# Attention of eight running samples: scores of samples 3 to 8 from rounded parts and rests

## What is computed

```python
def mla_sample(h, pos, c_ckv, c_kpe, ...):
    q_lat = jnp.einsum('bqhn,lhn->bqhl', q_nope, w_uk)
    s_past = (jnp.einsum('bqhl,bkl->bhqk', q_lat, c_ckv)
              + jnp.einsum('bqhr,bkr->bhqk', q_pe, c_kpe))
    s_new = (jnp.einsum('bqhl,bkl->bhqk', q_lat, ckv)
             + jnp.einsum('bqhr,bkr->bhqk', q_pe, kpe))
    sc = jnp.concatenate([s_past, s_new], axis=-1).astype(jnp.float32) * MLA_SCALE
    p = jax.nn.softmax(sc, axis=-1).astype(ckv.dtype)
    o_lat = (jnp.einsum('bhqk,bkl->bqhl', p[..., :past], c_ckv)
             + jnp.einsum('bhqk,bkl->bqhl', p[..., past:], ckv))
    o = jnp.einsum('bqhl,lhv->bqhv', o_lat, w_uv)...
```

## Time and profile before

| | us |
|---|---|
| median of 3 runs (1609.39 to 1609.46) | 1609.39 |
| span of the profiled execution | 1608.3 |
| PE busy in it | 1600.9 |
| DVE busy | 820.0 |
| ACT busy | 597.6 |
| POOL busy | 268.1 |

### The profile page before, as it was taken

How to read it: one execution, slowest core, us unless ns; L and a number is a source line. 1 busy time by engine, 2 the same in 40 slices (tenths; PEclk the granted TensorE clock), 3 DMA queues, 4 the chain that set the end, 5 groups by cost and what they waited for, 6 DMA issues and landing times.

```text
span 1608.3 us, 24111 instructions
## 1 busy us (share of the span) xinstructions
PE 1600.9 (100%) x9172; PEld 1532.5 (95%) x9172; DVE 820.0 (51%) x968; ACT 597.6 (37%) x770; POOL 268.1 (17%) x267
## 2 busy tenths in 40 slices
PE   9999999999999999999999999999999999999998
PEld 9999999988999999999999999898989899999987
DVE  6544344864454444445444344674747576444422
ACT  6333222574343333234333223424343354333322
POOL 0111122530121110221111032303030312111000
PEclk9999999999999999999999999999999999999999
DMA  7444344564244443454444345566575755444332
GB/s 218 121 121 130 105 126 135 173 206 148 58 126 130 130 127 94 126 150 131 130 123 120 104 125 186 204 219 228 198 245 172 254 179 147 130 130 130 113 125 103
DMA packets 322273, 238.03 MB, mean 148 GB/s; under 512 B 8560, under 2 KB 287280, under 8 KB 322096
## 3 DMA queue, kind: packets, MB, share of 16 engines
q1 hardware_dynamic: 321936, 236.86, 48.3%
q10 hardware_dynamic: 288, 0.50, 0.1%
HBM read 215.34 MB, written 20.94 MB: 147 GB/s over the span
## 4 chain that ended last, share of the span: by engine, by line
PE 98%; DVE 1%; ACT 1%; issue 0%; DMA 0%; ACTq 0%; DVEq 0%
PE bank L168 26%; PE bank L170 26%; PE bank L169 26%; PE bank L489 2%; PE bank L488 2%; PE bank L487 2%; PE bank L1666 1%; PE bank L1665 1%; PE bank L1664 1%; PE bank L1073 1%; PE bank L396 1%; PE bank L1702 1%; PE bank L1777 1%; PE bank L1733 1%; PE bank L1692 0%; PE bank L917 0%
## 5 line engine op out<-in xcount | busy, mean ns | idle before, releaser
L145 DVE TENSOR_TENSOR WL<-RAW,WH 128x2048 fp32r<-128x2048 f32 (+3 forms) x191 | 401.8, 2105 | 296.3 <-ACT WH L138 295.6
L138 ACT ACTIVATE WH<-RAW 128x2048 fp32r<-128x2048 f32 (+3 forms) x191 | 330.0, 1730 | 561.9 <-PE bank L170 479.5
L168 PE MATMUL bank<-XH,WH 128*128 128x384 f32 x1368 | 458.4, 335 | 0.0
L170 PE MATMUL bank<-XH,WL 128*128 128x384 f32 x1368 | 457.1, 334 | 0.0
L169 PE MATMUL bank<-XL,WH 128*128 128x384 f32 x1368 | 457.0, 334 | 0.0
L168 PEld LDWEIGHTS bank<-XH,WH 128*128 128x128 f32 x1368 | 256.8, 188 | 3.4 <-issue 3.1
L169 PEld LDWEIGHTS bank<-XL,WH 128*128 128x128 f32 x1368 | 256.8, 188 | 0.2
L170 PEld LDWEIGHTS bank<-XH,WL 128*128 128x128 f32 x1368 | 256.8, 188 | 0.0
L653 POOL TENSOR_TENSOR si<-si,rsb 128x384 f32<-128x384 f32 x88 | 94.3, 1072 | 626.4 <-ACT si L524 591.8
L168 PE MATMUL bank<-AH,WH 128*128 128x384 f32 x528 | 176.4, 334 | 0.0
L169 PE MATMUL bank<-AL,WH 128*128 128x384 f32 x528 | 176.4, 334 | 0.0
(11 more groups left out here) (307 smaller groups left out, 1960.3 us busy)
## 6 DMA issues: line engine op xcount, KB each, us to landing
RAW<-w_ffn_gate_dram SPq DMA_DIRECT2D x86, 512.0 KB, 4.0
RAW<-w_ffn_up_dram SPq DMA_DIRECT2D x86, 512.0 KB, 5.2
RAW<-w_ret_in_dram SPq DMA_DIRECT2D x48, 512.0 KB, 4.8
RAW<-w_ffn_down_dram SPq DMA_DIRECT2D x48, 384.0 KB, 4.0
st<-state_ret_dram SPq DMA_DIRECT2D x32, 512.0 KB, 6.9
new_state_sample_dram<-st SPq DMA_DIRECT2D x32, 512.0 KB, 6.6
RAW<-w_ffn_down_dram SPq DMA_DIRECT2D x48, 320.0 KB, 3.3
RAW<-w_ffn_down_dram SPq DMA_DIRECT2D x22, 512.0 KB, 4.3
```

Of the source, the lines that this page charges most:

```text
L138: ins = act.activation(dst(WH), src, ACT.Copy)
L145: ins = dve.tensor_tensor(dst(WL), src, dst(WH).bitcast(F32), ALU.subtract)
L168: pe.matmul(ps, wh, xh, start=first, stop=False)
L170: return pe.matmul(ps, wl, xh, start=False, stop=last)
```

## The change

- Keys of a sample now lie in one tile of three parts, two latent and one rotated (the 64 rotated rows twice, on both halves of the partitions), 128x3x528, and come in one transfer. There are four tiles in place of three.
- Both score banks now hold 272 keys. The banks are pairs that one instruction can read (`bank_pair`): samples take the up banks and the down banks in turn; the mixings use `norm_ps` and `misc_ps`.
- Samples 0 and 1 keep full-precision scores. For samples 2 to 7 (the third to the eighth) ACT rounds the keys (`keys_hi`) and the latent queries (`queries_hi`), DVE subtracts what was rounded off (`key_rest`, `query_rest`), in place, and PE makes 16 rounded matmuls of 272 columns for each sample. The rotated queries carry rounded part and rest on the two halves of the partitions.
- ACT rounds the keys of sample b+2 behind the exponentials of b. Behind them come the copies of the turned probabilities of b-2, and then the copy of the latents of b-3, which was DVE's.
- DVE takes one maximum over both banks; ahead of that of sample b stands the rest of the keys of b+1. ACT makes two exponentials in place of three.
- SP's queue issues all key loads first and then the latent rows of samples 4 to 7.
- Semaphores are merged (`consts_set`, `m_ps`, `m_negmax`).

The diff, cut to what is spoken of:

```diff
-                sp.dma_start(ktc[b % N_KT][:, :, 0:PAST_LEN], a["ckvT"][b]).then_inc(sem(f"kt_in{b % N_KT}"), 16)
-                sp.dma_start(ktp[b % N_KT][:, 0:HP], a["kpeT"][b]).then_inc(sem(f"kt_in{b % N_KT}"), 16)
+                sp.dma_start(keys_in[b % N_KT][:, :, 0:PAST_LEN], a["keysT"][b]).then_inc(sem(f"kt_in{b % N_KT}"), 16)
...
+                for b in range(N_KT, DEC_BATCH):
+                    sp.wait_ge(sem("m_sscores"), 2 * (b - N_KT + 1))
+                    self.load_keys(sp, b)
+                for b in range(NCB, DEC_BATCH):
+                    sp.wait_ge(sem("m_smixed"), b - NCB + 1)
+                    sp.dma_start(cc[:, b % NCB, :, :], a["ckv"][b]).then_inc(sem(f"cc_in{b % NCB}"), 16)
...
-            SA, SB, MIX = up_ps, (down_ps[0], norm_ps), (down_ps[1], misc_ps)
-            LAST_MIX = (misc_ps, norm_ps)
+            SCORES, MIX = bank_pair[1:3], (norm_ps, misc_ps)
+            LAST_MIX = (misc_ps, up_ps[0])
...
-                pe.matmul(sa, q0, latent[:, 0, HP:], start=True, stop=False)
-                pe.matmul(sa, q1, latent[:, 1, HP:], start=False, stop=False)
-                pe.matmul(sb_, q0, latent[:, 0, 0:HP], start=True, stop=False)
-                pe.matmul(sb_, q1, latent[:, 1, 0:HP], start=False, stop=False)
-                pe.matmul(sa, qr[0:ROPE, :], rotated[0:ROPE, :], start=False, stop=True).then_inc(sem("m_sscores"), 1)
-                pe.matmul(sb_, qr[ROPE:P, :], rotated[ROPE:P, 0:HP], start=False, stop=True).then_inc(sem("m_sscores"), 1)
+                if b >= SPLIT:
+                    n, hi, lo = b - SPLIT, key_hi[b % 2], key_lo[b % N_KT]
+                    for i, cols in enumerate(HALVES):
+                        for t in range(KV):
+                            pe.matmul(ps[i], lat_hi[:, t, n, :], hi[:, t, cols], start=(t == 0), stop=False)
+                            pe.matmul(ps[i], lat_hi[:, t, n, :], lo[:, t, cols], start=False, stop=False)
+                            pe.matmul(ps[i], lat_lo[:, t, b, :], hi[:, t, cols], start=False, stop=False)
+                        pe.matmul(ps[i], rot_q[:, n, :], hi[:, KV, cols], start=False, stop=False)
+                        pe.matmul(ps[i], rot_q[:, n, :], lo[:, KV, cols], start=False, stop=True).then_inc(sem("m_sscores"), 1)
+                    return
...
+                def keys_hi(b):
+                    act.wait_ge(sem(f"kt_in{b % N_KT}"), 16 * (b // N_KT + 1))
+                    act.wait_ge(sem("m_kt_new"), 2 * (b + 1))
...
+                    act.activation(key_hi[b % 2][:, :, :], keys_in[b % N_KT][:, :, :], ACT.Copy).then_inc(sem("m_split"), 1)
...
                 turned(MLA_HEADS - 1)
+                keys_hi(SPLIT)
+                act.wait_ge(sem("m_lat"), 4 * KV)
+                queries_hi(SPLIT, SPLIT + 3)
                 mixed(MLA_HEADS - 1)
...
                 for b in range(DEC_BATCH):
                     if b == 1:
                         new_rows()
+                    act.wait_ge(sem("m_snegmax"), 2 * (b + 1))
+                    act.wait_ge(sem("m_zero"), b + 1)
+                    scores = self.SCORES[b % 2]
+                    new = PAST_LEN + b * DEC_SEQ
+                    past = ps_[:, b % 2, PAST].rearrange("p (i n) -> p i n", i=2)
+                    for j, (dst, src) in enumerate(((past, scores[:, :, 0:HP]), (ps_[:, b % 2, new:new + DEC_SEQ], scores[:, 1, HP:KW]))):
+                        act.activation(dst, src, ACT.Exp, bias=stat[:, b % 2, 1:2], scale=MLA_SCALE,
+                                       accum_out=stat[:, b % 2, 2 + j:3 + j]).then_inc(sem("m_sexp"), 1)
+                    if b == 0:
+                        queries_hi(SPLIT + 3, DEC_BATCH)
+                    elif b + 2 < DEC_BATCH:
+                        keys_hi(b + 2)
                     if b >= 2:
                         turned_probs(b - 2)
-                    act.wait_ge(sem("m_snegmax"), b + 1)
-                    act.wait_ge(sem("m_zero"), b + 1)
-                    sa, sb_ = self.SA[b % 2], self.SB[b % 2]
-                    new = PAST_LEN + b * DEC_SEQ
-                    for j, (dst, src) in enumerate(((slice(0, HP), sa[:, 0:HP]), (slice(HP, PAST_LEN), sb_[:, 0:HP]),
-                                                    (slice(new, new + DEC_SEQ), sa[:, HP:KW]))):
-                        act.activation(ps_[:, b % 2, dst], src, ACT.Exp, bias=stat[:, b % 2, 2:3], scale=MLA_SCALE,
-                                       accum_out=stat[:, b % 2, 4 + j:5 + j]).then_inc(sem("m_sexp"), 1)
+                    if b >= 3:
+                        latents(b - 3)
...
+                def key_rest(b):
+                    dve.wait_ge(sem("m_split"), (1, 4, 5, 6, 7, 8)[b - SPLIT])
+                    dve.tensor_tensor(key_lo[b % N_KT][:, :, :], keys_in[b % N_KT][:, :, :], key_hi[b % 2][:, :, :].bitcast(F32),
+                                      ALU.subtract).then_inc(sem("m_rests"), 1)
...
                 for b in range(DEC_BATCH):
                     st = stat[:, b % 2, :]
-                    for j, (ps, n) in enumerate(((self.SA[b % 2], KW), (self.SB[b % 2], HP))):
-                        dve.wait_ge(sem("m_sscores"), 2 * b + 1 + j)
-                        dve.tensor_reduce(st[:, j:j + 1], ps[:, 0:n], AX.X, ALU.max).then_inc(sem("m_smax"), 1)
...
+                    if 2 <= b < DEC_BATCH - 1:
+                        key_rest(b + 1)
+                    dve.wait_ge(sem("m_sscores"), 2 * (b + 1))
+                    dve.tensor_reduce(st[:, 0:1], self.SCORES[b % 2][:, :, 0:KW], AX.XY, ALU.max).then_inc(sem("m_snegmax"), 1)
+                    dve.wait_ge(sem("m_snegmax"), 2 * b + 1)
+                    dve.tensor_scalar(st[:, 1:2], st[:, 0:1], -MLA_SCALE, None, ALU.mult).then_inc(sem("m_snegmax"), 1)
+                    if b == 0:
+                        key_rest(SPLIT)
+                        query_rest(SPLIT)
+                    elif 2 <= b < DEC_BATCH - 1:
+                        query_rest(b + 1)
+                    dve.wait_ge(sem("m_sexp"), 2 * (b + 1))
+                    dve.tensor_reduce(st[:, 4:5], st[:, 2:4], AX.X, ALU.add).then_inc(sem("m_ps"), 1)
...
-                    if b >= 3:
-                        mixed(b - 3)
-                for b in range(DEC_BATCH - 3, DEC_BATCH - 1):
-                    mixed(b)
...
+                for b in range(SPLIT, DEC_BATCH):
+                    if b + 1 < DEC_BATCH:
+                        new_keys(b + 1)
+                    zeros(b)
```

More of the change, by code:

```diff
@@ L83, in stream_kernel @@
         var = sb("var", [P, T])
+        with ExitStack() as r:
+            sq_split = sb("sq_split", [P, 2 * T], F32R, r)
         sq = sb("sq", [P, 2, T])
@@ L89, in stream_kernel @@
         accl = sb("accl", [P, T], F32R)
+        with ExitStack() as r:
+            bank_pair = [r.enter_context(nc.psum_tensor(f"bank_pair{i}", [P, 2, 512], F32)) for i in range(4)]
         bank = [ctx.enter_context(nc.psum_tensor(f"bank{i}", [P, 512], F32)) for i in range(8)]
@@ L711, in stream_kernel @@
             mcos, msin = mtab[:, 0:T], mtab[:, T:2 * T]
-            shared = sb("shared", [P, MLA_HEADS * T + KV * D_MODEL], F32, r)
+            widths = (MLA_HEADS * T + KV * D_MODEL, MLA_HEADS * T + MLA_HEADS * KV_LORA, 2 * KT, KV * DEC_BATCH * MLA_HEADS * DEC_SEQ)
+            with ExitStack() as r0:
+                whole = sb("whole", [P, sum(widths)], F32, r0)
+            with ExitStack() as r0:
+                split = sb("split", [P, sum(widths)], F32R, r0)
+            (shared, late, kt, lat), (shared_r, late_r, kt_r, lat_r) = (
+                [x[:, sum(widths[:i]):sum(widths[:i + 1])] for i in range(4)] for x in (whole, split))
+            r.enter_context(nc.sbuf_tensor("whole_held", [P, sum(widths)], F32))
             qn = shared[:, 0:MLA_HEADS * T].rearrange("p (h n) -> p h n", h=MLA_HEADS)
@@ new lines, in sample_scores @@
+                latent, rotated = keys_in[b], keys_in[b][:, KV, :]
+                for i, cols in enumerate(HALVES):
+                    pe.matmul(ps[i], q0, latent[:, 0, cols], start=True, stop=False)
+                    pe.matmul(ps[i], q1, latent[:, 1, cols], start=False, stop=False)
+                for i, cols in enumerate(HALVES):
+                    rows = slice(i * ROPE, (i + 1) * ROPE)
+                    pe.matmul(ps[i], qr[rows, :], rotated[rows, cols], start=False, stop=True).then_inc(sem("m_sscores"), 1)
@@ L1218, in turned_probs, with latents @@
                     act.activation(psT[:, b % 2, PAST], gate_ps[0][:, :], ACT.Copy).then_inc(sem("m_psT"), 1)
+                def latents(b):
+                    act.wait_ge(sem("m_smixed"), b + 1)
+                    act.activation(lat[:, :, b, :, :].rearrange("p t h q -> p t (h q)"),
+                                   self.MIX[b % 2][:, 0:KV * P].rearrange("p (t n) -> p t n", t=KV), ACT.Copy)\
+                       .then_inc(sem("m_olat"), 1)
                 for b in range(DEC_BATCH):
@@ L2172 @@
```

(3 more changed lines are left out.)

162 lines of the change are left out of this document (95 added, 67 removed).

## The result

The changed kernel takes 1627.1 us (median of 4 runs, 1626.51 to 1627.63), against 1609.4 for the kernel before: a ratio of 1.0109, 95% interval 1.0095 to 1.0123. It is 17.7 us slower. Forecast were 1628.0 and a range of 1620 to 1635.

What follows compares the result with a forecast made beforehand. PE was taken as the bound, made to wait for ACT's copies: span 1608.3 plus 15.6 of stalls (PE's saving included) plus 2.8 for the clock gives 1626.7; the median lies 1.1 above, so 1628.0 us, range 1620 to 1635.

Steps and rivals of the forecast that it cites:

- The likeliest case: Attention samples: PE's turnings stall for ACT's turned copies and the clock falls once; 1628.0 us, chance 0.50.
- The savings on PE: Scores of samples 2 to 7: rounded matmuls take 2.11 us instead of 2.53; PE's work alone falls by 2.4 us.
- The chain: End of scores through maximum, exponentials, rounding copy and turned copies holds each PE turning; delays sum to +15.6 us.
- Prices of the links: Costs per chain instruction: exponentials 1.03 us, rounding copy 1.53, turned copies 0.77, maximum and negation with handover 0.91.
- the last distance: From turning 6 to the values: order as before, latents copied by ACT cost at most 0.2 us.
- The subtraction: DVE's key subtraction, 1.87 us: on the path for keys 3 before turning 1; those of following samples cost nothing.
- The clock: PE drops to half rate after the first stall; turning 1 and mixing 0 cost 2.8 us more.
- The bound of 8: Upper bound on the clock's cost, 8 us, if the second stall drops it too and scores are caught.
- Costs set at nothing: Larger key loads, latent-row loads queued behind them on SP, and GpSimd's casts in idle time: no cost.
- more is lost: Rival: clock falls at both stalls (1631 to 1635), or weight loads are not hidden (1630 or 1633); chance 0.13.
- The fourth: Other side: the wait at the turnings is covered and only PE's 2.4 us count; 1607.0 us, chance 0.02.

Runs made afterwards that it cites:

- ahead: Changed kernel, reordered: ACT rounds keys b+2 before the exponentials of b, copies turned probabilities of b-1 after; DVE subtracts behind the negation; 1607.27 us.
- fill: Changed kernel plus 54 extra matmuls on PE, results unread, ahead of turnings 1 to 4 to keep it busy in the stalls; 1623.17 us.
- sub_behind: Changed kernel with only DVE's order altered: subtraction for keys b+1 goes behind the maximum and negation of b; 1624.33 us.
- turned_first: Changed kernel with ACT's copies of the turned probabilities of b-2 put back ahead of the exponentials of b; 1610.63 us.
- plain: Changed kernel with full-precision scores for all eight samples, no rounding copies or subtractions, and turned copies ahead of the exponentials; 1609.20 us.
- double_copy: Changed kernel with ACT making the rounding copy of keys 3 to 7 twice; 1636.55 us.
- turned_sub: Changed kernel with turned copies ahead of the exponentials on ACT and the key subtraction behind the negation on DVE; 1613.02 us.
- fill_first: Changed kernel with extra unread matmuls on PE in the first stall alone, ahead of turning 1; 1625.73 us.
- copy_last: Changed kernel with the rounding copy of keys b+2 moved behind the turned copies and latents on ACT; 1621.28 us.

## Why the prediction was right
The likeliest case came true by its mechanism: stalls at the turning, for ACT's copies, and a lower clock behind them. The sum came within 1 us in part by luck. On the span 15.6 + 2.8 = 18.4 us were forecast and 17.5 measured: the chain is 1.9 shorter than forecast, turning 0 starts 0.7 earlier than forecast, the clock costs 2.4 more, and 0.6 come back behind the attention.

- **The savings on PE** were right: 2.11 us forecast for the score passes, 2.1 measured, with weight loads hidden and the 13 ns of the earlier trace rows on top of the columns (272 columns at 2.4 GHz are 113 ns, measured 125). The Trainium skill, page "TensorE: Matmul & The Clock Gate", section "Back-to-back issue gap", would have them at an estimated 0.116; the change's trace, too, is 0.009 above it. What the forecast did not have: a sample without waits takes 4.78 us in ahead and not 5.40 - 0.42 = 4.98, since the turning and the mixing got shorter as well, by 0.08 and 0.10.
- **The chain** was right link by link and too long by 2 us. Summed, it was forecast at 53.5 us for the stretch and took 51.6 in fill, the run where nothing else acts. The step that was mis-sized is "Prices of the links". The rounding copy went in with its duration, 1.53, but ACT starts the next instruction 0.1 us before the copy ends: 1.41 from start to start in the rows above. The exponentials went in with 1.03; the two prices of the earlier trace rows, 0.68 and 0.25, are already from start to start and hold the reading, which was added once more: 0.93 measured. Four copies and five exponentials make 1.0 of the 1.9 us. The subtraction makes 0.14, the last distance 0.18 (the copy of latents on ACT costs nothing), and the rest is spread over the turnings (0.50 in place of 0.55) and handovers.
- **The subtraction** in the first stall was forecast with 1.87 and cost 1.73 from start to start; sub_behind shows it on the path there, while the stall of 4.23 behind it stays as it was. That later ones cost nothing held.
- **The clock** was forecast at 2.8 us for one fall and cost 5.2 for three. Both parts of that step were off: the one fall that was counted cost 1.4 and not 2.8, since the clock was back in the middle of mixing 0, and two more came, behind the stalls of 4.23 and 2.00 us, at 2.2 and 1.6. The bound of 8 held them.
- **Costs set at nothing** (larger key loads, latent rows behind them on SP's queue, GpSimd's casts) stayed so: turned_first and plain hold all of them and show no wait on PE for a load.
- Of the rivals, the second, "more is lost", had a condition met: the clock fell at both long stalls. Its 1631 to 1635 did not come, since even three falls cost 5.2 us, where it reckoned with up to 8 for two, and the chain was shorter. The fourth, that the wait would be covered, is what ahead makes true by another order. Its price was 1607.0 and 1607.3 was measured, again with two misses that cancel: ahead still waits 1.45 us at turnings 0 to 2, and PE saves 0.2 us more for each sample than was forecast.

## What to carry to other kernels
When a step is put into an in-order list, ask first whom the instructions behind it release: here 1.4 us of copying that ACT had plenty of time for stood, with a wait for the next sample's maximum, ahead of two copies that PE was waiting for. Put what releases the bound engine ahead of anything that waits on newer work, and look ahead with the new work in the gap in which the engine waits anyway. Count start-to-start distances along a chain, not durations, and price a long stall of the matmul engine above its own length: here stalls of 6.75 and 4.23 us cost 1.4 and 2.2 more by the clock.

## What the runs showed of the hardware
- The granted clock fell to half in or behind the stalls of 9.86, 6.75, 5.78, 5.33, 4.48 and 4.23 us. Among shorter ones length alone does not decide: it fell behind 3.34 (double_copy), 2.51 (turned_sub) and 2.00 (the change), and held behind 3.01 (double_copy), two of 2.00 each in fill_first and sub_behind and one of 2.82 (copy_last, where the score passes behind it start 0.125 apart). What does decide was not found. The fall need not come with the first matmul: in turned_sub the first four score matmuls behind the stall still start 0.13 us apart and the later ones 0.23. In the change a fall cost 1.4 to 2.2 us, by the distances with the stalls filled. The forecast had no fall for short stalls.
- Work that nobody reads is a remedy for it: 54 matmuls took 5.2 us off the stretch and 3.9 off the kernel's time.
- Entering rounded matmuls from full-precision ones costs 0.21 - 0.125, some 0.09 us, the same at 272 columns as at 384.
